# Four fp32 matrix products of the mLSTM and gMLP heads written as fp16 halves with three passes, and the state update put behind the fourth projection block

## The reference, cut to what matters

```python
# mLSTM, one head, chunks of tokens
qk  = einsum('bhtd,bhsd->bhts', q, k) * w                      # scores, times decays
num = inter * einsum('bhed,bhtd->bhte', C, q) + qk @ v
den = inter * einsum('bhd,bhtd->bht', n, q) + sum(qk)
h   = num / maximum(abs(den), exp(-mt))
C_new = decay * C + einsum('bhs,bhse,bhsd->bhed', ws, v, k)    # state update
n_new = decay * n + einsum('bhs,bhsd->bhd', ws, k)
# gMLP, one channel group: lower-triangular spatial gating
sp = einsum('gts,bcsgd->bctgd', tril(w_s), v) + b_s
out = gelu(u) * sp
```

## Time and profile before

| what | value |
|---|---|
| median of 3 runs | 991.31 us (990.66 to 992.35) |
| the profiled execution's own time | 991.04 us |
| its span, first to last instruction | 989.1 us |
| mean granted TensorE clock over the span | 0.995 |
| TensorE, weight load, VectorE, ScalarE, GpSimd busy | 97%, 76%, 82%, 68%, 2% |
| HBM traffic | 198.76 MB read, 204 GB/s over the span |
| head stage, layer 0 and layer 1 (from block 0 of head 0) | 41.1 us and 527.8 us on, four heads each |

### The profile page before, as it was taken

The page is one execution under the profiler, slowest core; times in us unless marked ns, Lnnn a source line. Parts: engine busy times, 40 slices in busy tenths (PEclk is TensorE's granted clock), DMA queues, the critical chain, the costliest instruction groups (busy, mean ns, idle before and its releaser), DMA issues.

```text
span 989.1 us, 24151 instructions
## 1 busy us (share of the span) xinstructions
PE 957.3 (97%) x9866; PEld 750.7 (76%) x9866; DVE 811.3 (82%) x1454; ACT 672.4 (68%) x1096; POOL 24.2 (2%) x38
## 2 busy tenths in 40 slices
PE   9999999999998999999999999999999989999995
PEld 6877777777776799976578777777777768999663
DVE  6796767786788899999888876778768879999995
ACT  7665454866355799877677545568653659998874
POOL 0000000000002000000100000000000020000002
PEclk9999999999999999999999999999999999999998
DMA  9855444323463299998736534442334424999971
GB/s 367 338 164 169 134 155 131 125 90 128 150 225 140 83 358 385 380 355 319 299 113 227 178 120 147 140 146 87 127 130 161 158 88 139 382 371 390 368 271 56
DMA packets 59653, 205.03 MB, mean 207 GB/s; under 512 B 7216, under 2 KB 10348, under 8 KB 59020
## 3 DMA queue, kind: packets, MB, share of 16 engines
q1 hardware_dynamic: 56748, 198.08, 55.7%
q10 hardware_dynamic: 2784, 5.28, 1.6%
HBM read 198.76 MB, written 3.40 MB: 204 GB/s over the span
## 4 chain that ended last, share of the span: by engine, by line
PE 71%; DVE 14%; ACT 8%; issue 5%; DVEq 1%; DMA 1%; ACTq 0%; SPq 0%
PE bank L1888 42%; DVE wlo L1146 9%; PE bank L1912 4%; ACT whi L603 4%; PE bank L2269 3%; PE bank L2437 2%; PE bank L1953 2%; PE bank L1917 1%; PE bank L2254 1%; PE bank L1961 1%; PE bank L2453 1%; PE bank L2186 1%; DVE arena_b L1827 1%; PE bank L2357 1%; PE bank L2054 1%
## 5 line engine op out<-in xcount | busy, mean ns | idle before, releaser
L1146 DVE SCALAR_TENSOR_TENSOR wlo<-w,whi 128x1024 f16<-128x1024 f32 x358 | 428.5, 1218 | 59.5 <-ACT whi L603 58.1
L603 ACT ACTIVATE whi<-w 128x1024 f16<-128x1024 f32 x358 | 371.2, 1051 | 84.2 <-PE bank L1888 53.0
L1888 PE MATMUL bank<-xhi,whi 128*128 128x320 f16 x688 | 206.1, 300 | 1.0 <-DVE wlo L1146 1.0
L1888 PE MATMUL bank<-xhi,wlo 128*128 128x320 f16 x688 | 205.7, 299 | 0.0
L1888 PE MATMUL bank<-xlo,whi 128*128 128x320 f16 x688 | 205.7, 299 | 0.0
L1888 PE MATMUL bank<-arena_b,whi 128*128 128x112 f16 x2048 | 159.3, 213 | 3.2 <-DVE wlo L1146 3.2
L1888 PE MATMUL bank<-arena_b,wlo 128*128 128x112 f16 x1024 | 156.0, 213 | 0.0
L1888 PEld LDWEIGHTS bank<-arena_b,whi 128*128 128x128 f16 x2048 | 149.8, 98 | 5.4 <-issue 3.1
L1888 PEld LDWEIGHTS bank<-arena_b,wlo 128*128 128x128 f16 x1024 | 100.2, 98 | 0.0
L1888 PEld LDWEIGHTS bank<-xhi,whi 128*128 128x128 f16 x688 | 67.2, 98 | 28.7 <-DVE wlo L1146 1.3
L1888 PEld LDWEIGHTS bank<-xhi,wlo 128*128 128x128 f16 x688 | 67.3, 98 | 26.2
(11 more groups left out here) (379 smaller groups left out, 1786.8 us busy)
## 6 DMA issues: line engine op xcount, KB each, us to landing
w<-in_w SPq DMA_DIRECT2D x358, 512.0 KB, 5.2
arena_b<-head_rows ACTq DMA_DIRECT2D x2, 1920.0 KB, 9.6
rows<-in_rows SPq DMA_DIRECT2D x2, 1024.0 KB, 9.8
xT<-in_x SPq DMA_DIRECT2D x2, 640.0 KB, 5.4
out_y<-xT SPq DMA_DIRECT2D x4, 320.0 KB
out_ckv<-arena_a SPq DMA_DIRECT2D x2, 320.0 KB
acc<-kr SPq DMA_DIRECT2D x2, 288.0 KB
arena_c<-kr SPq DMA_DIRECT2D x2, 288.0 KB
```

The costliest lines, as they stand in the source:

```text
L603: A(whi[:, n % SLOTS, :], w32[:, n % RAW, :], ACT.Copy, scale=WS).then_inc(hi_done.sem, 1)
L1146: V.scalar_tensor_tensor(wlo[:, n % SLOTS, :], w32[:, n % RAW, :], WS, whi[:, n % SLOTS, :], ALU.mult, ALU.subtract).then_inc(lo_done.sem, 1)
L1888: ins = M(out, w[:, s, sub * P:(sub + 1) * P], rhs(part, k), start=(n == 0), stop=(n == 3 * len(subs) - 1))
```

## The change

Only the head stage is touched. The transposes of k, the scores, the state update and the spatial gating no longer use fp32 operands. Each operand is split into an fp16 half and an fp16 remainder, and each product runs as three fp16 passes (half x half, half x remainder, remainder x half); the transposes become matmuls of each half with an fp16 identity. For that ScalarE writes second copies in fp16 (`mq_hi`, `mk_hi` in `evac`, `k_hi`, `k_lo`, `vw_hi`, `vg_hi`, `ws_hi`), and VectorE writes remainders (`mq_lo`, `mk_lo`, `vw_lo`, `vg_lo`, `ws_lo`). New signals `qk_lo`, `vw_h`, `vw_l`, `vg_h`, `vg_l`, `ws_h`, `ws_l` tie them together. Block 4 now runs ahead of the state update. On VectorE `vw_lo`, the gating tile and `lo_m(4)` now stand ahead of the state; the state itself takes two more instructions, since its scale must be undone. `latents_hi` and `latents_lo` are cut in two: the part for the cache and the gating weights stays in head 0, the part for the new latents moves to head 1.

```diff
@@ scalar
-                def latents_hi():
+                def cache_hi():
                         act.wait_ge(layer_in.sem, layer_in.value(l, 80))
                         A(kv_hi[:, :, 0:PAST], cache.rearrange("p (k t) -> p k t", k=2), ACT.Copy,
                           scale=XS).then_inc(c_hi.sem, 1)
+                        act.wait_ge(ws_masked.sem, ws_masked.value(l, 1))
+                        A(ws_hi[:, :], ws_t[:, :], ACT.Copy, scale=WS).then_inc(ws_h.sem, 1)
+
+                def latents_hi():
...
+                        if half is not None:
+                            A(half, bank[(M0 + step) % 4][:, 0:T], func, scale=scale * XS,
+                              bias=par_x[:, bass.ds(col, 1)])
                         A(dst, bank[(M0 + step) % 4][:, 0:T], func, scale=scale,
                           bias=par_t[:, bass.ds(col, 1)]).then_inc(z_ev.sem, 1)
...
-                    A(k_tok[:, 0:2, :], bank[4][:, 0:2 * P].rearrange("p (i n) -> p i n", i=2), ACT.Copy)
-                    A(k_tok[0:TS, 2, :], bank[4][0:TS, 2 * P:3 * P], ACT.Copy).then_inc(k_sb.sem, 1)
+                    for b, half in ((4, k_hi), (7, k_lo)):
+                        A(half[:, 0:2, :], bank[b][:, 0:2 * P].rearrange("p (i n) -> p i n", i=2), ACT.Copy)
+                        a = A(half[0:TS, 2, :], bank[b][0:TS, 2 * P:3 * P], ACT.Copy)
+                    a.then_inc(k_sb.sem, 1)
+                    act.wait_ge(v_wsd.sem, v_wsd.value(l, h + 1))
+                    A(vw_hi[:, 0:2, :], v_ws[:, 0:2, :], ACT.Copy, scale=XS)
+                    A(vw_hi[0:TS, 2, :], v_ws[0:TS, 2, :], ACT.Copy, scale=XS).then_inc(vw_h.sem, 1)
                     hi_m(3)
                     if h == 0:
+                        cache_hi()
+                    if h == 1:
                         latents_hi()
...
+                    act.wait_ge(vg_done.sem, vg_done.value(l, h + 1))
+                    A(vg_hi[:, 0:2, :], vg[:, 0:2, :], ACT.Copy, scale=XS)
+                    A(vg_hi[0:TS, 2, :], vg[0:TS, 2, :], ACT.Copy, scale=XS).then_inc(vg_h.sem, 1)
@@ vector
+                def cache_lo():
+                        dve.wait_ge(layer_in.sem, layer_in.value(l, 80))
+                        ws3 = ws_t[:, :].rearrange("p (n t) -> p n t", t=P)
+                        V.tensor_tensor(ws3, ws3, mats16[:, 1:2, :].broadcast_to([P, 4, P]), ALU.mult
+                                        ).then_inc(ws_masked.sem, 1)
                         dve.wait_ge(c_hi.sem, c_hi.value(l, 1))
...
+                        dve.wait_ge(ws_h.sem, ws_h.value(l, 1))
+                        V.scalar_tensor_tensor(ws_lo[:, :], ws_t[:, :], WS, ws_hi[:, :], ALU.mult, ALU.subtract
+                                               ).then_inc(ws_l.sem, 1)
...
                     V.tensor_tensor(q_in[:, :], mq[:, :], mrow_i[:, bass.ds(h * T, T)], ALU.mult)
+                    V.scalar_tensor_tensor(mq_lo, mq[:, :], XS, mq_hi, ALU.mult, ALU.subtract)
                     lo_m(2)
+                    dve.wait_ge(z_ev.sem, z_ev.value(l, h * 7 + 7))
+                    V.scalar_tensor_tensor(mk_lo, mk[:, :], XS, mk_hi, ALU.mult, ALU.subtract
+                                           ).then_inc(qk_lo.sem, 1)
...
                     lo_m(3)
                     if h == 0:
+                        cache_lo()
+                        dve.drain()
+                    if h == 1:
                         latents_lo()
-                        dve.drain()
...
+                    dve.wait_ge(vw_h.sem, vw_h.value(l, h + 1))
+                    V.scalar_tensor_tensor(vw_lo[:, 0:2, :], v_ws[:, 0:2, :], XS, vw_hi[:, 0:2, :], ALU.mult,
+                                           ALU.subtract)
+                    V.scalar_tensor_tensor(vw_lo[0:TS, 2, :], v_ws[0:TS, 2, :], XS, vw_hi[0:TS, 2, :], ALU.mult,
+                                           ALU.subtract).then_inc(vw_l.sem, 1)
...
+                    V.tensor_scalar(c_st[:, 0, :], bank[6][:, 0:W1], XS ** -2, None, ALU.mult)
+                    dve.drain()
+                    V.tensor_scalar(c_st[:, 5, :], c_st[:, 4, :], decay(T), None, ALU.mult)
+                    V.tensor_scalar(c_st[:, 3, :], c_st[:, 0, :], decay(TP), None, ALU.mult)
+                    dve.drain()
+                    V.scalar_tensor_tensor(c_st[:, 5, :], bank[6][:, 2 * W1:3 * W1], XS ** -2, c_st[:, 5, :],
+                                           ALU.mult, ALU.add)
+                    V.scalar_tensor_tensor(c_st[:, 3, :], bank[6][:, W1:2 * W1], XS ** -2, c_st[:, 3, :],
+                                           ALU.mult, ALU.add).then_inc(st_done.sem, 1)
...
+                    dve.wait_ge(vg_h.sem, vg_h.value(l, h + 1))
+                    V.scalar_tensor_tensor(vg_lo[:, 0:2, :], vg[:, 0:2, :], XS, vg_hi[:, 0:2, :], ALU.mult,
+                                           ALU.subtract)
+                    V.scalar_tensor_tensor(vg_lo[0:TS, 2, :], vg[0:TS, 2, :], XS, vg_hi[0:TS, 2, :], ALU.mult,
+                                           ALU.subtract).then_inc(vg_l.sem, 1)
@@ tensor
-                    for i, (t0, n) in enumerate(TILES):
-                        a = TR(bank[4][0:n, i * P:(i + 1) * P], mk[:, t0:t0 + n], ident[:, :])
+                    if h == 0:
+                        pe.wait_ge(cols_sb.sem, cols_sb.value(l, 1))
+                    pe.wait_ge(k_sb.sem, k_sb.value(l, h))
+                    pe.wait_ge(qk_lo.sem, qk_lo.value(l, h + 1))
+                    for b, half in ((4, mk_hi), (7, mk_lo)):
+                        for i, (t0, n) in enumerate(TILES):
+                            a = M(bank[b][0:n, i * P:(i + 1) * P], half[:, t0:t0 + n], mats16[:, 0, :], start=True,
+                                  stop=True)
                     a.then_inc(k_tr.sem, 1)
                     for i, (t0, n) in enumerate(TILES):
-                        a = M(bank[5][0:n, i * P:i * P + n], mk[:, t0:t0 + n], mq[:, t0:t0 + n],
-                              start=True, stop=True)
+                        for k, q in ((mk_hi, mq_hi), (mk_hi, mq_lo), (mk_lo, mq_hi)):
+                            a = M(bank[5][0:n, i * P:i * P + n], k[:, t0:t0 + n], q[:, t0:t0 + n],
+                                  start=(k is mk_hi and q is mq_hi), stop=(k is mk_lo))
                     a.then_inc(a_ps.sem, 1)
                     z_block(*zb(3, 6, 4))
+                    z_block(*zb(4, 7))
 
                     pe.wait_ge(k_sb.sem, k_sb.value(l, h + 1))
-                    pe.wait_ge(v_wsd.sem, v_wsd.value(l, h + 1))
-                    pe.wait_ge(cols_sb.sem, cols_sb.value(l, 1))
+                    pe.wait_ge(vw_l.sem, vw_l.value(l, h + 1))
                     pe.wait_ge(g_done.sem, g_done.value(l, h))
                     for c, (t0, n) in enumerate(TILES):
-                        a = M(bank[6][:, c * (DH + 1):(c + 1) * (DH + 1)], k_tok[0:n, c, :],
-                              v_ws[0:n, c, :], start=True, stop=True)
+                        for k, v in ((k_hi, vw_hi), (k_hi, vw_lo), (k_lo, vw_hi)):
+                            a = M(bank[6][:, c * (DH + 1):(c + 1) * (DH + 1)], k[0:n, c, :], v[0:n, c, :],
+                                  start=(k is k_hi and v is vw_hi), stop=(k is k_lo))
                     a.then_inc(dc_ps.sem, 1)
-                    z_block(*zb(4, 7))
                     z_block(*zb(5, 8))
...
-                    pe.wait_ge(vg_done.sem, vg_done.value(l, h + 1))
-                    pe.wait_ge(ws_masked.sem, ws_masked.value(l, 1))
+                    pe.wait_ge(vg_l.sem, vg_l.value(l, h + 1))
+                    pe.wait_ge(ws_l.sem, ws_l.value(l, 1))
...
+                        for v, w in ((vg_hi, ws_hi), (vg_hi, ws_lo), (vg_lo, ws_hi)):
+                            a = M(bank[6][:, t0:t0 + n], v[0:n, i, :], w[0:n, bass.ds(off, n)],
+                                  start=(v is vg_hi and w is ws_hi), stop=(v is vg_lo))
```

More of the change, by code:

```diff
@@ L189, in build_trunk @@
         mats16 = sb("mats16", [P, 3, P], F16)
+        ws_hi = sb("ws_hi", [P, 4 * P], F16)
+        ws_lo = sb("ws_lo", [P, 4 * P], F16)
+        vw_hi = sb("vw_hi", [P, 3, DH + 1], F16)
         slot_no = sb("slot_no", [P, CAP])
@@ L218, in build_trunk @@
         arena_c = sb("arena_c", [P, 15 * P + 3 * (DH + 1)])
-        k_tok, v_tok, dec_w, att, vg = (arena_c[:, 3 * P * n:3 * P * (n + 1)].rearrange(
-            "p (i n) -> p i n", i=3) for n in range(5))
+        v_tok, dec_w, att, vg = (arena_c[:, 3 * P * n:3 * P * (n + 1)].rearrange(
+            "p (i n) -> p i n", i=3) for n in range(1, 5))
         v_ws = arena_c[:, 15 * P:15 * P + 3 * (DH + 1)].rearrange("p (i n) -> p i n", i=3)
+        ysq16 = ysq[:, :, :].rearrange("p a t -> p (a t)").bitcast(F16)
+        vg_hi, vg_lo = (ysq16[:, 3 * P * n:3 * P * (n + 1)].rearrange("p (i n) -> p i n", i=3) for n in range(2))
+        mq_hi, mq_lo, mk_hi, mk_lo = (ysq16[:, 6 * P + T * n:6 * P + T * (n + 1)] for n in range(4))
+        vw_lo = ysq16[:, 6 * P + 4 * T:6 * P + 4 * T + 3 * (DH + 1)].rearrange("p (i n) -> p i n", i=3)
```

(28 more changed lines are left out.)

51 lines of the change are left out of this document (22 added, 29 removed).

## The result

The changed kernel takes 999.61 us (median of six, 997.99 to 1003.11), the kernel before beside it 991.74 (990.66 to 992.58): ratio 1.008, 95% interval 1.0066 to 1.0093. It is slower by some 8 us where I had forecast no change (991.0, range 987.3 to 995.0) and had given slower a chance of 0.25. The profiled execution of the changed kernel took 998.21 us with a span of 996.2, that of before 991.04, so 7.2 us are to be found in these two traces.

The account below looks back on a forecast made before the run. TensorE, busy 97% of the span, was taken as the bound; 10.3 us saved over eight heads, set against the new waits, left -0.3 us from the median 991.31, so 991.0 us, range 987.3 to 995.0.

Parts of the forecast that it names:

- What TensorE saves: Head stage's transposes, scores, state update and gating: 2.99 us in fp32 to 1.70 in fp16, saving 1.29 us a head.
- My own bound: Head-stage matmuls: if short ones cost as much as long ones, the saving would be 1.13 us a head.
- The sign that the saving was not there: Heads 2 and 3 staying at 31.4 us from first block to first block, where 30.4 was forecast.
- The other sign that came true: A stretch at granted clock 0.50 in the head stage would show the forecast wrong.
- First wait, mk_lo: TensorE waits before the transposes for VectorE's k remainder: 2.3 us lost in head 0, 0.27 in each other head.
- Second wait, vw_lo: TensorE's state update waits for the state weights' remainder: just in time, about 0.05 us lost in head 0.
- Third wait, the new state: TensorE waits before the numerator for VectorE's state: 0.96 us lost in head 0, 0.87 in head 1, none later.
- Sum: Head 0 +2.0 us, head 1 -0.15, heads 2 and 3 -1.0 each; two layers -0.3 us.
- Rival C, the clock: TensorE's clock drops in head 0 after the new pause: 1.7 us in each layer, 994.4 us; chance 0.06.
- Rivals B: VectorE's state chain, vw_lo to the state's last add, later than reckoned: one microsecond more gives 995.0 us; chance 0.16.
- D: SP's queue delays block 27's load behind four loads and the key rows: 5 us late gives 1001; chance 0.03.
- The bands: Uncertainty of the whole sum: -2.5 / +3 us, including -0.1 to +0.5 a layer for signals into TensorE.

Follow-up runs that it names:

- the rearranged one: Changed kernel with transposes and scores ordered for two shape changes, VectorE's halves made earlier, key rows' transfer later in SP's queue: 987.21 us, 0.9952 of the kernel before.

## Why the prediction was wrong

- **"What TensorE saves", 1.70 us in fp16: the step that failed.** Measured 2.75, so the saving is 0.24 us a head, 1.9 and not 10.3 in all: 8.4 us. What was missing is a term, 0.105 us for each of the ten changes of shape in a head. The prices were right for matmuls that follow one of their own shape (0.76 us with no change of shape, as forecast; the 0.44 for gating should by the same prices be 0.42). I took them from a run of 64 equal matmuls and three equal short ones and put them on groups that change shape ten times. My own bound ("were the short ones as dear as the long ones, 1.13 a head") varied the columns and not the neighbours, so the range couldn't hold what came. The sign that the saving was not there was named: heads 2 and 3 at 31.4; they last 31.49. The other sign that came true is the stretch at clock 0.50.
- **First wait, mk_lo: right.** 2.31 us in head 0 forecast; the transposes start 2.46 us after the last matmul of the value block where 0.06 is the normal step, 2.40. 0.27 in the others; the step there is 0.38, 0.32.
- **Second wait, vw_lo: right that it is nothing** (0.05), though in part for another reason: vw_lo ends at 61.46 (forecast 61.3), and TensorE comes at 62.05, 0.7 us later than reckoned. In the kernels that bring TensorE earlier it appears, 0.48 and 0.94 us idle.
- **Third wait, the new state: its time was right, the loss was not.** The last add ends at 66.08 (forecast 66.05), but TensorE wants it only at about 66.0, since its fp16 groups took longer. 0.2 us are lost in head 0 of layer 0 and none elsewhere, where 0.96 was forecast for head 0 and 0.87 for head 1 of each layer: 3.5 us less in both layers. So part of the failed step (3.5 of 8.4 us) was repaid by this one: time that TensorE does not save also hides a wait. That the total is no further off is luck, not foresight.
- **Sum.** 8.4 of saving not there, less 3.5 of waits not there, plus 0.5 of the first wait above the forecast, 1.6 of clock, 0.2 of numerators that ran slower in three heads (0.52 against 0.44 us to the first product of the state; why is open), 0.4 outside the heads: 7.6, against 7.4 between the profiled execution and the 990.8 forecast for it.
- **Rival C, the clock, got 0.06 and happened.** A pause of 2.24 us did what I thought it too short for, in one of the two layers of the profiled execution. Its price was right (1.7 forecast, 1.6 measured). It gives 1.6 of the 7.2 us there, and by the estimate above some 3 of the 8 us between the six runs and the kernel before. The trace of before already said that the clock is a matter of chance: the same pause of 2.7 us stands at 317.79 and at 804.31, and only the second brought a stretch at 0.50. The prediction uses the second alone.
- **Rivals B and D did not happen.** The state chain was on time (66.08 against 66.05). SP's queue: TensorE's waits for weight remainders come to 4.1 us in the whole kernel before, 3.9 in the changed and 3.6 in the rearranged one, so no late load shows.
- **The bands were too narrow** for another reason than scatter: I put the unknown at +0.5 a layer of signals, and on the largest term of the sum only at 0.16 us a head (1.29 or 1.13).

## What to carry to other kernels

Price a group of short matmuls by its sequence, not by its count: here 0.056 us for each of 128 columns that follows one of its own active rows and columns, and some 0.11 us more for every change. So gather the ragged tiles of several groups; giving them the full shape took 0.22 us less still, but was only tried in a kernel that computes other values. When fp32 becomes three fp16 passes, the halves are new operands at the end of VectorE's queue: put each right behind its source, ahead of work that has slack, and reckon the queue again after each saving, since a wait that was hidden by the old cost appears when the cost goes. Reckon a pause of 2 us and more on TensorE at its length and, with some chance, 1.7 us of clock. Read single starts in a narrow window: groups and busy time hide the price of a change of shape.

## What the runs showed of the hardware that was not expected

- A weight load whose active rows or columns differ from those of the matmul ahead does not start beside it, but some 0.15 us after that matmul's start (94.10 to 94.25); from 128 to 64 columns, from 128 to 64 rows, and back. Seen in fp16, with 64 to 320 moving columns. In fp32 the state update pays as well (0.20 us in place of 0.11 between starts at 56.49 and 56.69), the transposes do not. What in the array asks for it was not tried.
- A pause of 2.2 us on TensorE is followed by a stretch at granted clock 0.50 in some executions and not in others: in the four profiled kernels that have it (two heads each) in five heads of eight. Behind pauses of 1.65 us and less there is none as long as TensorE has work. Behind the pause of 2.7 us at the first layer norm of each layer (near 318 and 808 us) there is one in 13 cases of 20 over the ten profiles. The stretch is 3.4 us, in two cases 6.8, and costs half of it. The Trainium skill, page "TensorE: Matmul & The Clock Gate", section "Why this matters for your kernels", has pauses between bursts bring the lower clock back; the traces agree that they do, and show that one and the same pause does so only sometimes.
